# One transformer layer on one core: table products in four strips, values of the dilated sample attention a step earlier, and the last scores of the selected attention ahead of the seventh sequence's values

## The chip, the cores and the metric

The kernel runs on one core of a Trainium2 chip. The metric is the device time of one execution in microseconds (us). The median of three runs before the change is 2094.52 us (2089.33 to 2097.07).

## The reference, cut to what matters

One layer is computed for a prompt (1024 rows of width 1024) and for eight sequences that each decode four new rows on top of 8192 cached positions. In outline:

```python
qa, ka, va, qb, kc, vc, ksl, vsl, kw, vw, gates = _mix_inputs(x, norm_attn, w_in)   # RMS norm, then x @ w_in
o_a = dilated attention over the last 2048 positions (steps 1, 4, 16), 8 heads, bias from rel_bias
o_cmp, p = attention over blocks of 64 positions, compressed by a small MLP
o_slc = attention over the 16 best blocks by p          # the "choice"
o_win = attention over the last 512 positions
x = x + [o_a, gate(o_cmp, o_slc, o_win)] @ w_out ; x = x + conv/gelu feed-forward
```

`rel_bias` has 32 buckets for 16 heads. The kernel turns it into three tables (one bias per head and distance, with a mask): a one-hot matrix of 35 rows times `rel_bias`.

## The kernel before, in words

**The order of the program.** `hybrid_step` writes one program for five engines and their queues. Its stages are `front` (norm, transposes, tables, the product with `w_in`, compression), `compressed_and_dilated` (sample and prompt attention over compressed blocks, and the sample's dilated attention), `sample_selected` (selected and window attention of the eight sequences), `prompt_attention` and `ffn`. Each engine runs its own list in order; semaphores join them. TensorE (PE) writes into eight banks of PSUM; VectorE (DVE) and ScalarE (ACT) copy the banks out.

**Opening of `front`.** Nine tiles of input rows are squared and summed (ACT, `squares`), three tiles at a time get their root (`root`), DVE scales each tile (`scaled`), PE turns each in two halves (jobs "x", L579) and ACT or DVE copies each half out (`moved`). Between them stand thirteen jobs "b" (L570): products of 512 columns of the one-hot table with the bias (16 output rows each), five ahead of tile 0, four ahead of tile 3, four ahead of tile 6, each copied out on its own. PE takes all jobs in one order over five banks; job j waits until job j-5 is copied. Afterwards SP stores the tables in scratch memory (L515 to L519) and the product with `w_in` begins (L588, L601).

**`compressed_and_dilated`.** Steps s = 0 to 11 are a loop that each engine follows. In step s PE turns the 8 key tiles of sequence s (`keys`, L1546) in two halves through two PSUM banks (`psT`), which ACT (even tiles) and DVE (odd tiles) copy out; a third tile can only be turned when the first is copied. `scores` (L1568) multiplies queries and turned keys. Four sequences form a group g. After a group: maximum (DVE), exponential (ACT), `probs(g)` (L1580, turned probabilities through the same two banks), `values(g)` (L1594, 256 small matmuls), `out(g)`. Before the change `probs` stands at steps 5 and 9 and `values` at the start of steps 6 and 10. Between these steps stand parts of the compressed attention: on DVE `prompt_maxima` and `block_probs` in step 4 (L1829 to L1843), `prompt_weights` and `choice` in step 5 (L1847 to L1871).

**Loads of that stage.** SP loads 16 items (keys or values of one sequence, 1.8 MB each in five DMAs, L167 to L172) into seven slots, in the order of `turns`: keys of sequences 0 to 5 (items 0 to 5), values 0 to 3 (items 6 to 9), keys 6 and 7 (10, 11), values 4 to 7 (12 to 15). Items 0 to 4 are loaded in `front`. Slot 5 holds a bias until `d_ab` is 2 and slot 6 another until `selected_bias` is done (`d_rp` is 4). Item i waits until item i-7 is used (`free_after`). SP's list goes on with the choice, `cache_win_k`, eight stores of the compressed output (`mixc`, L1514) and `cache_win_v`. POOL issues the first gathers of the next stage (`gather_keys`, L157), two after the last keys are turned and two after `values(1)`.

**`sample_selected`.** For each sequence b and quarter c: a gather of 1 MB of keys and one of values by POOL (L157, L2131), six buffers each; PE turns the keys (L2249), multiplies them (L2260), turns the probabilities of the sequence before (`probs`, L2270) and multiplies its values (L2288). The last step is `merge`, with the values of the last sequence.

## Time and profile before

| | |
|---|---|
| median of three runs | 2094.52 us (2089.33 to 2097.07) |
| the profiled execution | 2091.84 us, its span 2090.0 us |
| PE busy in the span | 97% |
| DVE, ACT, POOL busy | 53%, 25%, 28% |
| opening (until the product with `w_in` starts) | 0 to 40.74 us |
| rest of `front` | 40.74 to 503 us |
| `compressed_and_dilated` on PE | 503 to 613 us |
| `sample_selected` on PE | 613 to 794 us |
| `prompt_attention` and `ffn` | 794 to 2090 us |

All times of the profile come from one execution, in us from the start of its span. "Idle before" is time in which the engine did nothing ahead of a row, with what ended it; "issue" means that the profile shows nothing that it waited for. The granted clock is TensorE's, as a share of full speed.

### The profile page before, as it was taken

The numbers are of one execution on the slowest core, as the hardware profiler recorded it, in microseconds if no ns is written. First come the engines' busy times: TensorE is split into PE (matmuls) and PEld (weight loads), VectorE is DVE, ScalarE is ACT, GpSimd is POOL, SyncE is SP. The second block draws the span as 40 slices with busy tenths as digits, with TensorE's granted clock in tenths as the row PEclk, the third lists the DMA queues.
The fourth block names the chain that finished last, engine by engine and source line by source line (L and its number), as shares of the span: only waits on it lengthen the run. The fifth ranks groups of instructions, "written<-read, shape, count | busy, mean of one in ns | idle before, by whom it ended". The sixth has DMA issues, their size and how long they took to land. (4 is left out here: it accounts for less than half of the span.)

```text
span 2090.0 us, 31740 instructions
## 1 busy us (share of the span) xinstructions
PE 2030.1 (97%) x12334; PEld 1325.8 (63%) x12334; DVE 1113.5 (53%) x2524; ACT 520.4 (25%) x1140; POOL 578.9 (28%) x753
## 2 busy tenths in 40 slices
PE   7999999999989989999999999999999999999998
PEld 3445466666556666766776458888888888634443
DVE  4035455421535546777775467777776766511452
ACT  4111010101333435776675031111111111000001
POOL 2444234202025740112232441322222222304110
PEclk9999999999999999999999999999999999999999
DMA  9376677663699994233343126666665422601111
GB/s 255 118 237 258 263 289 277 242 214 124 229 365 387 419 409 162 70 92 92 93 143 112 29 81 221 221 211 213 218 205 202 142 81 62 242 4 30 43 40 41
DMA packets 154296, 373.04 MB, mean 178 GB/s; under 512 B 34885, under 2 KB 92989, under 8 KB 136093
## 3 DMA queue, kind: packets, MB, share of 16 engines
q1 hardware_dynamic: 126420, 149.63, 22.8%
q0 software_dynamic: 25472, 149.45, 18.4%
q10 hardware_dynamic: 2256, 71.94, 9.8%
q8 instruction: 99, 1.62, 0.3%
q14 instruction: 49, 0.40, 0.1%
HBM read 343.68 MB, written 98.60 MB: 212 GB/s over the span
## 5 line engine op out<-in xcount | busy, mean ns | idle before, releaser
L2981 PE MATMUL ff_ps<-ff_hx,whole_aw 128*128 128x264 f32 x2464 | 550.5, 386 | 0.8 <-DVE ff_hx L3377 0.8
L2981 PEld LDWEIGHTS ff_ps<-ff_hx,whole_aw 128*128 128x128 f32 x2464 | 467.1, 190 | 80.6 <-issue 1.2
L837 DVE STREAM_TRANSPOSE whole_space<-whole_space 128x512 f32<-128x512 f32 x256 | 155.3, 674 | 153.6 <-PE late_bank L637 153.6
L601 PE MATMUL late_bank<-in_w,in_xT 128*128 128x512 f32 (+1 forms) x512 | 201.6, 547 | 0.0
L1224 DVE CUSTOM_DVE_ANT_0 pa_L<-late_bank,whole_space 128x512 f32<-128x512 f32 (+3 forms) x288 | 141.0, 532 | 43.4 <-PE late_bank L1070 41.8
L601 PEld LDWEIGHTS late_bank<-in_w,in_xT 128*128 128x128 f32 x512 | 95.1, 191 | 95.0 <-issue 88.4
L1196 ACT ACTIVATE pa_L<-pa_L,pa_nm 128x640 f32<-128x640 f32 (+3 forms) x192 | 142.0, 741 | 47.0 <-DVE pa_nm L1236 46.7
L3007 PE MATMUL ff_ps<-ff_hx,whole_space 128*128 128x512 f32 x336 | 148.0, 593 | 0.0
L717 ACT ACTIVATE in_yout<-late_bank 128x128 f32<-128x128 f32 (+5 forms) x88 | 40.9, 479 | 380.7 <-PE late_bank L601 200.2
L3461 DVE SCALAR_TENSOR_TENSOR whole_space<-whole_space,ff_kept 128x1024 f32<-128x1024 f32 x88 | 123.1, 1399 | 3.1
L637 PE MATMUL late_bank<-whole_space 128*64 128x256 f32 (+1 forms) x1152 | 121.6, 364 | 0.0
L615 PE MATMUL late_bank<-in_xT,in_w 128*128 128x352 f32 x384 | 117.6, 463 | 0.0
L3220 ACT ACTIVATE whole_space<-whole_space 128x1056 f32<-128x1056 f32 x22 | 23.8, 1083 | 367.2 <-DVE whole_space L3463 367.2
L3007 PEld LDWEIGHTS ff_ps<-ff_hx,whole_space 128*128 128x128 f32 x336 | 63.6, 190 | 80.6 <-issue 80.6
L1091 PE MATMUL late_bank<-whole_ident,pa_L 128*128 128x128 f32 x816 | 113.4, 281 | 0.9
L1091 PEld LDWEIGHTS late_bank<-whole_ident,pa_L 128*128 128x128 f32 x816 | 87.5, 141 | 41.9 <-ACT pa_L L1196 18.4
L1111 PE MATMUL late_bank<-pa_PT,whole_space 128*64 128x128 f32 x1632 | 110.3, 279 | 0.9 <-DVE pa_tmp L1266 0.5
L637 PEld LDWEIGHTS late_bank<-whole_space 128*64 128x64 f32 x1152 | 74.8, 137 | 47.2 <-issue 13.0
L1070 PE MATMUL late_bank<-whole_space,pa_qT 64*128 64x512 f32 (+3 forms) x528 | 104.0, 498 | 0.0
L1190 ACT ACTIVATE pa_PT<-late_bank 128x512 f32<-128x512 f32 (+2 forms) x174 | 86.7, 536 | 54.4 <-PE late_bank L1091 53.4
L615 PEld LDWEIGHTS late_bank<-in_xT,in_w 128*128 128x128 f32 x384 | 71.8, 190 | 42.2 <-issue 3.8
L1111 PEld LDWEIGHTS late_bank<-pa_PT,whole_space 128*64 128x64 f32 x1632 | 87.2, 136 | 16.6 <-issue 13.0
(441 smaller groups left out, 2670.0 us busy)
## 6 DMA issues: line engine op xcount, KB each, us to landing
out_new_a_k_s<-in_cache_a_k ACTq DMA_DIRECT2D x8, 4088.0 KB
out_new_a_v_s<-in_cache_a_v ACTq DMA_DIRECT2D x8, 4088.0 KB
whole_aw<-in_w_up SPq DMA_DIRECT2D x44, 512.0 KB, 7.4
in_w<-in_w_in SPq DMA_DIRECT2D x5, 2048.0 KB, 13.0
whole_space<-in_cache_a_k SPq DMA_DIRECT2D x8, 1024.0 KB
whole_space<-in_cache_a_v SPq DMA_DIRECT2D x8, 1024.0 KB
ff_hx<-in_w_down SPq DMA_DIRECT2D x14, 512.0 KB, 4.2
whole_space<-in_x_prompt SPq DMA_DIRECT2D x12, 512.0 KB, 10.2
```

The source lines that it names most:

```text
L601: mm = pe.matmul(ps[0:n, b, 0:width], xT[:, k, t * P:t * P + n], w[:, at % WBUF, k, 0:width], start=(k == 0), stop=(k == KC - 1))
L615: mm = pe.matmul(ps[:, b, 0:n], w[:, at % WBUF, k, c * P:c * P + P], xT[:, k, r0:r0 + n], start=(k == 0), stop=(k == KC - 1))
L637: mm = pe.matmul(psH[dh * HD:dh * HD + HD, r % 2, o0:o0 + n], w1[:, kv, t16, dh, :], rows[:, dh, t, :], start=(t16 == 0), stop=(t16 == 15) ...
L837: last = dve.transpose(put[:, dh, :, k * HD:k * HD + HD].rearrange("p t (g b) -> p t g b", g=2), got[:, :, :, dh, :])
L1070: pe.matmul(psS[:, c % 2, h, 0:w], q, kT[i][r, j0 * P + k0:j0 * P + k0 + w], start=True, stop=True).then_inc(s_qk, 1)
L1091: mm = pe.transpose(psT[:, b % 3, (x - x0) * P:(x - x0) * P + P], turned, ident[:, :])
L1111: mm = pe.matmul(psO[h * HD:h * HD + HD, u % 2, 0:P], V[i][:, j0 + j, v0:v0 + HD], PT[:, u % 3, (2 * j + h) * P:(2 * j + h) * P + P], star ...
L1196: nc.scalar.activation(x, x, ACT.Exp, bias=nm[:, s, h:h + 1], scale=1.0, accum_out=sm[:, s, h:h + 1]).then_inc(s_ex, 1)
L1224: dve.tensor_tensor_reduce(L[:, u % 3, h, 512 * x:512 * x + n], psS[:, c % 2, h, 0:n], T[it % 2][:, h, SEQ - w + 512 * x:SEQ - w + 512 * x ...
L2981: mm = pe.matmul(ps[:, bank_of(x, j, g), 0:H2], aw[:, j % 2, at, k, :], hx[:, bt, k, g * H2:g * H2 + H2], start=(k == 0), stop=(k == KH - 1))
L3007: mm = pe.matmul(ps[:, b, :], a[:, k, :], wd(k0 + k)[:, c0:c0 + 512], start=(k == 0), stop=(k == KD - 1))
L3461: dve.scalar_tensor_tensor(out=out[:, 0:SEQ], in0=U[:, v, k:k + SEQ], scalar=tap(k), in1=out[:, 0:SEQ], op0=ALU.mult, op1=ALU.add)
```

## The change

Four edits, all in the order of work; no arithmetic is added or removed.

1. The thirteen table products become four jobs ahead of all tiles. Each job writes three or four products into one bank, in strips of 32 output rows, and is copied out once. The tiles follow without table jobs between them; who copies what, and when, is written out anew for ACT and DVE. The tables are stored by ten DMAs instead of seven.
2. SP loads the items in the order 5, 7, 8, 9, 10, 6, 11 to 15, and stores the choice behind item 15. `cache_win_v` is loaded behind the keys of sequence 6, ahead of `cache_win_k` and the `mixc` stores.
3. `probs(0)` moves from the end of step 5 to the end of step 4, `values(0)` from the start of step 6 into step 5, between `keys(5, 0)` and `scores(4, 1)`. Each of a group's four sequences now counts `d_pv` up, so that a slot, and the first gathers, are free after one sequence's values.
4. In `sample_selected` the last quarter's scores of the last sequence stand ahead of `values` of sequence 6; ACT copies those values out after the first two exponentials of the last sequence.

```diff
@@ front @@
+    NBJ = 4
+    jobs = [("b", m) for m in range(NBJ)]
+    first_x = len(jobs)
+    for t in range(NTILE):
+        jobs += [("x", t, 0), ("x", t, 1)]
...
+                    for k in range(job[1], len(chunks), NBJ):
+                        i, c = chunks[k]
+                        o, strip = tables[i][1] + c * CH, k // NBJ * 32
+                        mm = pe.matmul(ps[strip:strip + 32, b, :], relx[:, i, :], tab_op[:, o:o + CH], start=True, stop=True,
+                                       tile_position=(0, strip))
...
             squares(2)
             root(0)
             moved(0)
+            moved(2)
+            turned(0, 0)
             squares(3)
+            turned(1, 0)
             squares(4)
...
             squares(5)
...
             root(1)
+            turned(2, 0)
+            turned(2, 1)
+            turned(3, 0)
             squares(6)
+            turned(4, 0)
             squares(7)
             squares(8)
...
             root(2)
+            turned(5, 0)
...
+            moved(1)
             mean_square(0)
+            scaled(0)
             moved(3)
+            scaled(1)
+            turned(0)
+            scaled(2)
+            turned(1)
             mean_square(1)
+            scaled(3)
+            scaled(4)
+            turned(3)
@@ compressed_and_dilated @@
-            pool.wait_ge(d_tr, use["keys", NB - 1, NTL - 1] + 1)
-            pool.wait_ge(d_pv, 1)
+            pool.wait_ge(d_pv, 4)
             for c in range(2):
                 pre.gather_keys(pool, 0, c)
+            pool.wait_ge(d_tr, use["keys", NB - 1, NTL - 1] + 1)
             ahead.retire()
             pool.sem_inc(ops.s_retired, 1)
-            pool.wait_ge(d_pv, 2)
+            pool.wait_ge(d_pv, 5)
...
-            for i in range(5, 12):
+            for i in (5, 7, 8, 9, 10, 6, 11, 12, 13, 14, 15):
...
             sp.wait_ge(s_v, 17)
...
-            for i in range(12, 16):
-                load(i)
...
+            sp.wait_ge(d_tr, use["keys", NB - 2, NTL - 1] + 1)
+            pre.load_window(sp, "cache_win_v", pre.value, pre.s_wv)
...
-                mm.then_inc(d_pv, 1)
+                    mm.then_inc(d_pv, 1)
...
             for s in range(NB + 4):
+                if s == 10:
+                    values(1)
                 for g in range(2):
-                    if s == 6 + 4 * g:
-                        values(g)
...
                 if s < NB:
                     keys(s, 0)
+                if s == 5:
+                    values(0)
                 if 1 <= s <= NB:
                     scores(s - 1, 1)
...
-                    if s == 5 + 4 * g:
+                    if s == turning[g]:
                         probs(g)
@@ sample_selected @@
-                    if 0 <= n < NB * NQ:
+                    if 0 <= n < NB * NQ - 1:
                         scores(n // NQ, n % NQ)
+                    if n == NB * NQ - 2:
+                        scores(NB - 1, NQ - 1)
...
```

`turning` is (4, 9). ACT's and DVE's parts of `probs` move with it; DVE's copy of `probs(0)` then stands between its key copies of step 4 and `prompt_maxima`.

## Rows read from the trace of the kernel before

**Rows 1.** The page: busy time of the engines in the span.
```profile
PE 2030.1 (97%) x12334; PEld 1325.8 (63%) x12334; DVE 1113.5 (53%) x2524; ACT 520.4 (25%) x1140; POOL 578.9 (28%) x753
```
**Rows 2.** Timeline of PE in the opening: start, us, instruction, count, idle before.
```profile
24.77 3.60 PE L570 MATMUL late_bank<-in_yout,in_relx 35*16 35x512 f32 x8
28.30 2.84 PE L579 MATMUL late_bank<-whole_ident,whole_space 128*128 128x128 f32 x24
31.07 4.51 PE L570 MATMUL late_bank<-in_yout,in_relx 35*16 35x512 f32 x8
35.51 4.66 PE L579 MATMUL late_bank<-whole_ident,whole_space 128*128 128x128 f32 x24
40.74 3.64 PE L588 MATMUL late_bank<-in_w,in_xT 128*32 128x512 f32 x16 [0.57 <-ACT in_xT L717]
```
**Rows 3.** Timelines of ACT and of DVE in the opening.
```profile
14.70 1.04 ACT L724 ACTIVATE sample_kcs<-whole_space 128x1024 f32<-128x1024 f32 x1
...
16.59 3.68 DVE L799 SCALAR_TENSOR_TENSOR whole_space<-whole_space,in_rstd,sel_BS 128x1024 f32<-128x1024 f32 x3 [0.27 <-ACT in_rstd L729]
...
24.22 0.68 DVE L803 TENSOR_SCALAR in_xT<-late_bank 128x512 f32<-128x512 f32 x1
```
**Rows 4.** Timeline of PE, `compressed_and_dilated`, steps 3 to 5.
```profile
539.71 1.00 PE L1546 MATMUL late_bank<-whole_ident,whole_space 128*128 128x128 f32 x8 [0.25 <-ACT sample_turned L1739]
...
550.80 0.99 PE L1546 MATMUL late_bank<-whole_ident,whole_space 128*128 128x128 f32 x8 [1.13 <-ACT sample_turned L1739]
...
554.15 3.41 PE L1546 MATMUL late_bank<-whole_ident,whole_space 128*128 128x128 f32 x16
...
564.36 8.14 PE L1594 MATMUL late_bank<-whole_space,cd_PT 128*32 128x128 f32 x256
```
**Rows 5.** Timeline of DVE, same steps: first and last of two groups.
```profile
551.92 1.21 DVE L1829 TENSOR_REDUCE cd_mxp<-cd_Lp 128x64 f32<-128x1024 f32 x1
...
554.73 0.48 DVE L1843 TENSOR_SCALAR cd_early<-cd_early,cd_rcs 128x128 f32<-128x128 f32 x2
...
564.19 1.20 DVE L1847 TENSOR_REDUCE cd_smp<-cd_Lp 128x64 f32<-128x1024 f32 x1
...
569.41 0.22 DVE L1871 TENSOR_SCALAR cd_pen<-cd_score 64x128 f32<-64x128 f32 x1
```
**Rows 6.** Stretches of 5 us: PE, PEld, DVE, ACT, POOL busy, clock, DMA share, GB/s.
```profile
525.00:530.00 5.00, 5.00 (x100) 3.55 (x96) 0.69 (x1) 1.05 (x2) 0.00 (x0) 1.00 0.00 0
...
565.00:570.00 5.00, 5.00 (x170) 4.07 (x160) 4.31 (x15) 0.00 (x0) 0.00 (x0) 1.00 0.03 7
...
655.00:660.00 5.00, 4.27 (x105) 3.89 (x94) 0.53 (x1) 0.97 (x3) 1.21 (x2) 1.00 0.48 197
...
785.00:790.00 5.00, 4.00 (x121) 3.43 (x124) 3.29 (x10) 0.31 (x1) 0.00 (x0) 0.97 0.42 172
```
**Rows 7.** Timeline of SP's queue: items 6 and 12, first rows.
```profile
531.30 1.84 SPq L167 DMA_DIRECT2D whole_space<-in_cache_a_v  x3
...
570.37 1.99 SPq L167 DMA_DIRECT2D whole_space<-in_cache_a_v  x3
```
**Rows 8.** Timeline of POOL: the first gather of the next stage.
```profile
588.85 1.01 POOL L157 DMA_INDIRECT whole_space<-in_cache_slc_k,sample_idx  x1 [72.91 <-PE late_bank L1546]
```
**Rows 9.** Timeline of PE: second part of `values(1)`, window keys, first keys that waited.
```profile
606.93 5.43 PE L1594 MATMUL late_bank<-whole_space,cd_PT 128*32 128x128 f32 x117 [2.79 <-issue]
...
614.06 4.02 PE L2185 MATMUL late_bank<-whole_ident,whole_space 128*128 128x128 f32 x32
...
637.92 3.19 PE L2249 MATMUL late_bank<-whole_ident,whole_space 128*128 128x128 f32 x16 [2.25 <-DMA whole_space<-in_cache_slc_k,sample_idx]
```
**Rows 10.** Timelines of PE and of POOL: end of `sample_selected`.
```profile
778.41 1.06 PE L2260 MATMUL late_bank<-whole_space,sample_Qb 128*32 128x512 f32 x8
781.63 3.76 PE L2270 MATMUL late_bank<-whole_ident,sb_work 128*128 128x128 f32 x16 [2.15 <-ACT sb_work L2413]
...
779.29 0.94 POOL L2131 DMA_INDIRECT whole_space<-in_cache_slc_v,sample_idx  x1 [15.12 <-PE late_bank L2291]
```

More of the change, by code:

```diff
@@ L267, in front @@
     chunks = [(i, c) for i, (_, _, ln) in enumerate(tables) for c in range(ln // CH)]
-    shares = [chunks[0:5], chunks[5:9], chunks[9:13]]
-    jobs = []
-    for g in range(NG):
-        jobs += [("b", i, c) for i, c in shares[g]]
-        for t in range(3 * g, 3 * g + 3):
-            jobs += [("x", t, 0), ("x", t, 1)]
+    NBJ = 4
+    segments = []
+    for k, (i, c) in enumerate(chunks):
+        if c == 0 or k % NBJ == 0:
+            segments.append([i, c, k // NBJ, k % NBJ, 0])
+        segments[-1][4] += 1
+    NTS = len(segments) + A0 // FARW
+    jobs = [("b", m) for m in range(NBJ)]
+    first_x = len(jobs)
+    for t in range(NTILE):
+        jobs += [("x", t, 0), ("x", t, 1)]
     NX = len(jobs)
@@ L294, in front @@
     span_of = {ch: [j for j, x in enumerate(jobs) if x[0] in "nsq" and x[1] == ch] for ch in range(6)}
-    first_x = {g: min(j for j, x in enumerate(jobs) if x[0] == "x" and x[1] == 3 * g) for g in range(NG)}
     last_b = max(j for j, x in enumerate(jobs) if x[0] == "b")
@@ L299, in front, with by_act @@
     kT_row = {0: 0, 2: 8, 3: 10}
-    on_act = [j >= NX or j % 2 == 0 for j in range(NJ)]
+    def by_act(j):
+        if j < first_x:
+            return j % 2 == 0
+        return j >= NX or jobs[j][2] == 0 or jobs[j][1] % 3 == 2
+    on_act = [by_act(j) for j in range(NJ)]
     def done(j):
@@ L690, in copy_out @@
             if job[0] == "b":
-                _, i, c = job
-                o = res_at[i] + c * CH
-                return copy(res[:, o:o + CH], ps[0:HA + HB, b, :], 1.0)
+                n = 32 * len(range(job[1], len(chunks), NBJ))
+                return copy(res[0:n, job[1] * CH:job[1] * CH + CH], ps[0:n, b, :], 1.0)
             if job[0] == "x":
@@ L755, in _, with turned @@
             nc.scalar.activation(bias[:, 0:1], bias[:, 0:1], ACT.Sqrt)
+            def turned(t, h):
+                moved(first_x + 2 * t + h)
             squares(0)
@@ L856, in _, with turned @@
             dve.wait_ge(s_one, 2)
+            def turned(t):
+                moved(first_x + 2 * t + 1)
+            moved(1)
             mean_square(0)
-            for t in range(3):
-                scaled(t)
-            moved(1)
+            scaled(0)
             moved(3)
+            scaled(1)
+            turned(0)
+            scaled(2)
+            turned(1)
             mean_square(1)
-            for t in range(3, 6):
-                moved(2 * t - 1)
-                scaled(t)
-            moved(11)
-            moved(13)
-            mean_square(2)
-            for t in range(6, 9):
-                moved(2 * t + 3)
-                scaled(t)
-            for j in range(21, NX, 2):
-                moved(j)
+            scaled(3)
+            scaled(4)
+            turned(3)
+            scaled(5)
+            turned(4)
+            mean_square(2)
+            scaled(6)
+            scaled(7)
+            turned(6)
+            scaled(8)
+            turned(7)
             indices()
@@ L905, in _ @@
             pool.memset(ss[:, :], 1.0).then_inc(s_one, 1)
+            pool.memset(relx[:, :, HA + HB:32], 0.0).then_inc(s_one, 1)
             pool.memset(w2, 0.0).then_inc(s_wz, 1)
```

62 lines of the change are left out of this document (30 added, 32 removed).

## The prediction

> **What bounds the kernel now.** I read the page first, then stretches of 5 us of the two sample stages, then the timelines of single engines where PE or the DMA engines pause. PE is busy 97% of the span [rows 1], so a change of order can win only at its pauses, at its stretches of low clock, or where the DMA engines dictate. Three places are touched.
>
> In the opening PE is not what ends it. Tile 3 is scaled by DVE before PE has finished the second batch of table products, which runs until 28.4, and tile 6 waits in the same way until 35.5; then the last three tiles take until 40.2 and the product with `w_in` starts at 40.74 [rows 2]. From there to 503 us PE has no pause to speak of, so what the opening wins should go through.
>
> In `compressed_and_dilated` PE is near its limit: small waits for a bank, and one of 1.13 us after which keys ran slowly, 3.41 us for sixteen transposes [rows 4] where 32 others took 4.02 [rows 9]. The DMA engines pause twice: at 525 to 530 and at 565 to 570 nothing moves [rows 6]. With their flanks these pauses are 10.6 us and 9.8 us (idle shares of the 5 us stretches around those two, summed). The first ends when SP is let past item 6 at 531.30, the second when item 12 goes out at 570.37, behind the choice [rows 7]. From about 580 on the DMA engines are full until the gathers end, but for 2.6 us at 655 to 660 [rows 6]. So the end of `sample_selected` is the end of a stream of bytes: it moves by the pauses filled or made, not by how early one load is issued.
>
> **The change part by part, against the profiled execution, 2091.84 us (2.7 us under the median of the runs).**
>
> *Opening.* Two batches of 3.60 and 4.51 us leave PE's list between tiles [rows 2]. The four strips of a job should overlap: 16 matmuls of L588 with 32 output rows took 3.64 us [rows 2], 0.23 us each, where eight of L570 took 3.60, 0.45 each, although L588 ran right after an idle stretch, at a low clock. Four jobs ahead of the tiles then take about 7 us from 9.93, done before the first tile is scaled at 17.8, so they are hidden; the cover is the wait for the input rows. What remains is a chain of ACT and DVE. Nine squares at 1.04, scaling at 1.2 a tile (3.68 for three) and copies of 0.6 to 0.7 [rows 3], followed through the new lists by hand: root 1 at 24.4, tiles 3 to 5 scaled by 29.7; squares 6 to 8 now stand behind copies and end at 31.7, root 2 at 32.2, tile 8 scaled at 36.6, copied at 38.1. The product starts at 38.4 instead of 40.74: -2.3. If PE's transposes all ran at the low clock (twice the 2.84 for three tiles' 24 [rows 2]) they would take 1.9 us a tile, and it would be about -1. I take -2, ends -3 and 0. Three more table stores on SP, and a memset on POOL, lie beside 60 us in which nothing waits for them: nothing.
>
> *Step 4.* DVE now waits in its list for `probs(0)` before `prompt_maxima` and `block_probs`. Those are 3.3 us in one piece, 551.92 to 555.21 [rows 5], done so far while PE worked on scores and on keys of step 5. Now they start near 556.5 and end near 560. PE can turn three tiles of `keys(5)`, then needs DVE's copy of the second: it stands from about 558 to 560.5. +2.5 us, ends 0 and +3.3.
>
> *Step 5.* `prompt_weights` and `choice` are 5.4 us of DVE, 564.19 to 569.63 [rows 5], and lay wholly under `values(0)`, 8.14 us from 564.36 [rows 4]. With `values(0)` moved ahead of `keys(5, 1)` DVE idles under it, then has these 5.4 us, the scaling of the output (0.75) and a key copy (0.7) in front of PE's fourth tile of `keys(6)`. Behind `keys(5, 1)` PE has 0.95 of scores, 1.0 of block sums and three tiles, 1.6: 3.5 us. It stands 6.9 - 3.5 = +3.4 us; ends 0 (if the lists slip past each other) and +4.
>
> *Clock.* After the pause of 1.13 us sixteen transposes took 1.4 us too long [rows 4]; after one of 2.79 the 117 matmuls of `values(1)` took 5.43 instead of about 3.9 [rows 9]. Two new pauses can cost up to 3 us, or nothing beyond what is slow there already: +1.5.
>
> *Loads.* Items 7, 8 and 9 fill the first pause, 520 to 535; item 10 must wait for the keys of sequence 3, turned at 540.7 [rows 4], and item 6 stands behind it: about 5 us of new pause. Item 11 is in by 557; item 12 needs the keys of sequence 5, which PE now turns after `values(0)`: near 571 to 575. The two early gathers (at 588.85 before [rows 8]) go out when `values(0)` is done, near 568 to 570, and cover 5 us. That leaves 12 us empty. Later there may be 3 us more while SP waits for the choice to be read back. The sum of pauses is about 20, as it was (20.4): the loads are moved, not gained. Nothing for them, ends -3 and +3.
>
> *Start of `sample_selected`.* PE arrives 2.5 + 3.4 + 1.5 = 7.4 us later in its own account. It had waited there for gathered keys, 2.25 us [rows 9] and 0.5 more, with 1.6 us lost to the low clock behind it (3.19 for 2.0, and 0.4 on the scores). These 4.3 us it need not wait again. So +7.4 - 4.3 = +3.1 at the point where its first values free buffers for POOL, which is where the 2.6 us of DMA pause lie [rows 6]; this swallows the rest. The stream ends about +3.
>
> The second part of `values(1)` was held for 2.79 us by "issue", with the DMA engines full; `values(0)`, the same 256 matmuls with the DMA engines empty, ran through in 8.14 [rows 4, 9]. In the new order `values(0)` meets them empty again and `values(1)` full again, since window loads and `mixc` stores lie just ahead. I leave both as they are.
> The Trainium skill (Runtime: NRT & Kernel Launch, Instruction fetch mechanics) says that an engine's instructions come in blocks of 256 over a DMA queue of its own; by this the pause is a late block, and would go, 2.8 us, only if the DMA engines had room at that place. The trace fits with it, but shows no block.
>
> *Tail.* With the last scores ahead of `values` of sequence 6, the wait of 2.15 us before the last `probs` [rows 10] and its slow 3.76 us (some 2.0 for sixteen at full clock) could go: -3.9 at best. But the last two value gathers are released by the end of those values, at 779.29 [rows 10], and now 1.1 us later; they were landing until about 787 (0.42 of the stretch from 785 [rows 6]). The last values would start near 782 and wait for them. I take -1.5, ends -3.9 and +1.
>
> Sum: -2 + 3 - 1.5 = -0.5 us; 2091.84 becomes about 2091.3. The runs' median stands 2.7 higher; I write 2092.
>
> **The rivals.** *The pauses shrink.* If DVE's two blocks of work slip into gaps, if `values(1)` finds its instructions in time (2.8 and 1.5 of clock), and with -3 and -3.9 at the ends, the time is 2091.84 - 3 - 4.3 - 3.9 + 0 = about 2080.5. For it: both DMA pauses are real, and the gathers do start 20 us earlier. Against it: the 5.4 us of DVE need a cover of PE work that is no longer there. The rule on instruction blocks belongs here.
>
> *DVE becomes the bound in steps 4 to 6.* Both waits at full size and each followed by some 3 us at 1.2 GHz instead of 2.4: 3.3 + 4 + 3 = 10.3 us; if the item loads behind them are late by as much, nothing of the 4.3 comes back, and with an opening and a tail of nothing it is 2102. It decides if `keys(6)` begins after 583, against 572.5, the end of `values(0)`, before [rows 4]. For it: two PSUM banks and one order on DVE leave no way round. Against: 7 to 8 us of the DMA backlog at 613 are there to absorb it.
>
> *The strips do not overlap.* Thirteen products one after another at the low clock, 1.74 each, would end at 32.5, and the tiles would follow from there: about +11, 2103. L588 speaks against it, though it has 128 rows of operand and not 35.
>
> **How the numbers follow.** Near nothing (2086 to 2098): 0.53. Pauses shrink: 0.24, of which three quarters lie beyond 0.5% (10.5 us, about what a measurement of this kernel can tell from no change). DVE the bound: 0.18, nearly half of it beyond. Strips: 0.05, all beyond. That gives faster 0.19, slower 0.13, same 0.68. For eight in ten I reach into both neighbours, 2082 to 2101: the ends of the unsure terms alone (loads 3 either way, clock 1.5, opening 1 to 2, tail 2.5) make some 6 us each way.
>
> **What would show it.** In the changed kernel: L588 starts at 38 to 39; PE stands before the fourth tile of `keys(5)` for 2 to 3 us, ended by DVE, and again before the fourth of `keys(6)` for about 3.4; `prompt_weights` starts after `values(0)` and not under it; the DMA engines are empty for about 12 us before 570; no keys of L2249 wait more than 1 us before 650; in the tail the wait before the last L2270 is gone and one of 1 to 2 us stands inside the last L2288. I am wrong if `keys(6)` begins before 575, or if PE reaches the window keys (614.06 before [rows 9]) more than 3 us earlier.

## The result, and the profile after

Six runs of the changed kernel gave 2102.9 us in the median (2102.49 to 2108.17), six of the kernel before, on the same chip, 2092.5 (2087.34 to 2097.07): ratio 1.005, 95% interval 1.0032 to 1.0068, so 0.5% slower, about 10.4 us. The forecast was 2092, with a range that ended at 2101. The profiled run took 2103.95 us, its span is 2102.2, 12.2 more than before. The page's line of busy times answers to [rows 1]:

```profile
PE 2030.0 (97%) x12334; PEld 1330.5 (63%) x12334; DVE 1115.1 (53%) x2517; ACT 519.4 (25%) x1138; POOL 578.7 (28%) x754
```

PE is busy for as long as before in total, so the 12.2 us are time in which it stands.

The opening went as forecast. The timeline of PE (start, us, instruction, count, idle before), first the row of the kernel before at the same place, which [rows 2] lack:

```profile
9.93 8.71 PE L570 MATMUL late_bank<-in_yout,in_relx 35*16 35x512 f32 x10 [9.93 <-DMA in_relx<-in_c_pick]
```

In the changed kernel:

```profile
10.56 7.04 PE L581 MATMUL late_bank<-in_yout,in_relx 35*32 35x512 f32 x26 [10.56 <-DMA in_relx<-in_c_pick]
...
37.69 3.64 PE L600 MATMUL late_bank<-in_w,in_xT 128*32 128x512 f32 x16 [0.56 <-ACT in_xT L728]
```

The strips overlap: 13 products (26 halves) take 7.04 us, 0.54 each, where the first five took 8.71, 1.74 each. The product with `w_in` starts at 37.69 instead of 40.74 [rows 2]; of these 3.05 us, 2.0 are left at the first keys of the dilated stage (500.92 against 502.93).

From there all is lost again. PE in steps 4 to 6 and up to the window keys:

```profile
555.42 0.70 PE L1572 MATMUL late_bank<-whole_ident,whole_space 128*128 128x128 f32 x4
556.34 1.14 PE L1572 MATMUL late_bank<-whole_ident,whole_space 128*128 128x128 f32 x8 [0.21 <-DVE cd_PT L1946]
560.15 1.11 PE L1572 MATMUL late_bank<-whole_ident,whole_space 128*128 128x128 f32 x4 [2.67 <-DVE sample_turned L1762]
561.19 10.27 PE L1620 MATMUL late_bank<-whole_space,cd_PT 128*32 128x128 f32 x256
...
582.25 0.66 PE L1572 MATMUL late_bank<-whole_ident,whole_space 128*128 128x128 f32 x4 [3.17 <-DVE sample_turned L1762]
...
625.05 0.39 PE L2207 MATMUL late_bank<-whole_ident,sample_knew 32*128 32x32 f32 x2 [4.27 <-DMA whole_space<-in_cache_win_k]
625.37 6.29 PE L2213 MATMUL late_bank<-whole_ident,whole_space 128*128 128x128 f32 x32
```

The two waits for DVE stand where the forecast had them, 2.67 and 3.17 us. New is the line before the last: PE waits 4.27 us for `cache_win_k` and begins the window keys 11 us later than before [rows 9]; there it waited for nothing. `values(0)`, 8.14 us before [rows 4], takes 10.27 after its pause.

The stretches of 5 us (PE, PEld, DVE, ACT, POOL busy, clock, DMA share, GB/s):

```profile
535.00:540.00 5.00, 4.62 (x39) 2.92 (x41) 2.13 (x4) 1.94 (x4) 0.00 (x0) 0.99 0.00 2
...
560.00:565.00 5.00, 4.85 (x72) 3.58 (x76) 0.78 (x2) 0.00 (x0) 0.00 (x0) 0.50 0.01 2
565.00:570.00 5.00, 5.00 (x152) 4.14 (x156) 0.00 (x0) 0.00 (x0) 0.00 (x0) 0.92 0.01 3
570.00:575.00 5.00, 4.75 (x74) 2.77 (x63) 0.69 (x1) 0.60 (x1) 1.99 (x2) 1.00 0.21 39
...
600.00:605.00 5.00, 4.91 (x18) 1.51 (x17) 2.70 (x5) 1.81 (x3) 0.00 (x0) 1.00 0.46 125
...
625.00:630.00 5.00, 4.95 (x24) 4.91 (x25) 1.61 (x3) 1.26 (x3) 1.44 (x2) 0.50 0.70 250
630.00:635.00 5.00, 5.00 (x69) 3.68 (x68) 1.66 (x4) 2.46 (x4) 1.92 (x3) 0.93 0.20 32
```

Two things are to be read here. The DMA pause of before at 525 to 530 [rows 6] is filled, but the last column but one shows new ones: the idle shares of all stretches from 520 to 605, summed, are 26.6 us, against 20.5 before, and 5.5 more follow at 625 to 635. (The 2.6 us of before at 655 to 660 [rows 6] are gone; from 520 to 665 the sums are 32.3 and 23.4.) And the clock column shows 0.50, that is 1.2 of 2.4 GHz, in two stretches behind pauses of PE: `values(0)` and the 32 transposes of the window keys (6.29 us instead of the 4.02 of [rows 9]) run slowly.

The pause at 625 to 635 is made by PE's lateness. The window keys lie in buffers that the next gathers need, and POOL waits for their transposes:

```profile
632.47 0.97 POOL L157 DMA_INDIRECT whole_space<-in_cache_slc_k,sample_idx  x1 [6.04 <-PE late_bank L2213]
```

Why the window keys are late is in SP's queue. Before, it had these rows:

```profile
569.65 0.67 SPq L1502 DMA_DIRECT2D scr_pen<-cd_pen  x1
...
588.00 1.74 SPq L151 DMA_DIRECT2D whole_space<-in_cache_win_k  x2
```

In the changed kernel:

```profile
575.39 2.20 SPq L167 DMA_DIRECT2D whole_space<-in_cache_a_v  x3
...
592.67 0.66 SPq L1529 DMA_DIRECT2D scr_pen<-cd_pen  x1
601.48 0.56 SPq L140 DMA_DIRECT2D sample_kcs<-scr_pen  x1
...
604.21 1.05 SPq L151 DMA_DIRECT2D whole_space<-in_cache_win_k  x2
```

Item 12 goes out at 575.39 (570.37 before [rows 7]). The penalties' store, which stood ahead of item 12, now stands behind item 15, at 592.67, and it is 8.8 us later that SP, which waits for it to land, reads the choice back. `cache_win_k` is issued 16.2 us later than before.

In the tail the wait before the last `probs` is gone, as forecast, but inside the last values there are two:

```profile
797.99 1.08 PE L2316 MATMUL late_bank<-whole_space,sb_PT 128*32 128x128 f32 x32 [1.48 <-DMA whole_space<-in_cache_slc_v,sample_idx]
801.07 1.71 PE L2316 MATMUL late_bank<-whole_space,sb_PT 128*32 128x128 f32 x32 [2.00 <-DMA whole_space<-in_cache_slc_v,sample_idx]
...
804.88 3.62 PE L2340 MATMUL late_bank<-sb_stackW,sample_vcs 128*128 128x32 f32 x16 [0.72 <-DVE sb_stackW L2549]
```

and the last line, 1.97 us in the kernel before, is slow behind them. From the last keys to the first product of the prompt's attention it takes 25.1 us, 22.4 before.

### The profile page after: what moved, and what is told of

Its sections match the earlier page's. It is cut to its first block and busy times, and to the rows that moved or that the text cites. A ratio compares the mean times of both kernels' runs of the same rounds, so it can differ in the third digit from the quotient of the medians.

```text
span 2102.2 us, 31736 instructions
## 1 busy us (share of the span) xinstructions
PE 2030.0 (97%) x12334; PEld 1330.5 (63%) x12334; DVE 1115.1 (53%) x2517; ACT 519.4 (25%) x1138; POOL 578.7 (28%) x754
## 5 line engine op out<-in xcount | busy, mean ns | idle before, releaser
L1117 PEld LDWEIGHTS late_bank<-whole_ident,pa_L 128*128 128x128 f32 x816 | 87.3, 141 | 42.1 <-ACT pa_L L1222 18.2
L1137 PE MATMUL late_bank<-pa_PT,whole_space 128*64 128x128 f32 x1632 | 110.3, 279 | 0.9 <-DVE pa_tmp L1292 0.5
```

The source lines that it names most:

```text
L1117: mm = pe.transpose(psT[:, b % 3, (x - x0) * P:(x - x0) * P + P], turned, ident[:, :])
L1137: mm = pe.matmul(psO[h * HD:h * HD + HD, u % 2, 0:P], V[i][:, j0 + j, v0:v0 + HD], PT[:, u % 3, (2 * j + h) * P:(2 * j + h) * P + P], star ...
```

## Experiments

All 15 were timed against the kernel before on the same chip, but not all on one chip: e1 to e4, e5 to e8, e9 to e12 and e13 to e15 are four groups. Inside a group medians can be compared; across groups, and with the changed kernel, only the ratios. The window keys' begin is the clearest mark in the traces. Since the profiled executions reach the dilated stage up to 5 us apart, I count in this section from the first keys of `compressed_and_dilated` in each trace (502.93 before, 500.92 changed). "out(1)" is the begin of PE's last product ahead of the window keys, which takes 0.66 us; if the window keys begin later than 0.6 us behind it, PE waited for their load.

| kernel | ratio to before (95%) | median, us | choice read back | out(1) | window keys begin | prompt attention begins |
|---|---|---|---|---|---|---|
| before | 1 | 2090.2 to 2092.5 | 82.5 | 110.3 | 110.9 | 291.1 |
| changed | 1.0050 (1.0032, 1.0068) | 2102.9 | 100.6 | 119.2 | 124.1 | 307.5 |
| e1 opening alone | 0.9984 (0.9970, 0.9999) | 2088.1 | 81.3 | 107.8 | 108.4 | 291.3 |
| e2 tail alone | 1.0010 (0.9998, 1.0023) | 2094.5 | 81.7 | 110.0 | 110.5 | 295.0 |
| e3 sample stages alone | 1.0049 (1.0032, 1.0066) | 2100.6 | 97.4 | 116.9 | 121.3 | 301.1 |
| e4 loads alone | 0.9982 (0.9969, 0.9995) | 2087.5 | 87.7 | 109.5 | 110.1 | 286.9 |
| e12 e4, item 12 held | 1.0039 (1.0022, 1.0055) | 2098.5 | 95.0 | 106.2 | 118.7 | 298.1 |
| e5 changed, POOL stores pen | 1.0016 (1.0000, 1.0032) | 2094.9 | 87.2 | 117.1 | 117.7 | 298.5 |
| e6 changed, DVE covered | 1.0047 (1.0029, 1.0066) | 2099.5 | 93.7 | 109.5 | 118.7 | 299.4 |
| e8 e5 and e6 | 1.0028 (1.0015, 1.0042) | 2096.9 | 84.9 | 109.7 | 116.2 | 299.2 |
| e7 changed, values(0) back | 1.0037 (1.0026, 1.0048) | 2098.6 | 94.2 | 113.5 | 118.0 | 301.3 |
| e11 changed, win_k first | 1.0023 (1.0010, 1.0037) | 2095.9 | 97.3 | 117.4 | 117.9 | 301.6 |
| e13 changed, gathers late | 1.0068 (1.0056, 1.0081) | 2107.3 | 95.1 | 117.3 | 124.4 | 308.3 |
| e14 e8 and e11 | 0.9986 (0.9975, 0.9998) | 2088.1 | 85.6 | 110.9 | 111.4 | 290.4 |
| e9 opening and loads | 0.9983 (0.9965, 1.0000) | 2085.9 | 86.5 | 108.9 | 109.5 | 288.3 |
| e10 e9, spare buffers | 0.9966 (0.9952, 0.9979) | 2083.6 | 87.4 | 108.4 | 109.0 | 283.4 |
| e15 e10, POOL stores pen | 0.9943 (0.9928, 0.9958) | 2081.4 | 86.2 | 109.9 | 110.5 | 285.0 |

**The parts alone.** e1 has the hunks of `front` only, e2 those of `sample_selected`, e3 those of `compressed_and_dilated`. e4 is e3 with PE's order as before:

```diff
-        turning = (4, 9)
+        turning = (5, 9)
...
-                if s == 10:
-                    values(1)
                 for g in range(2):
+                    if s == 6 + 4 * g:
+                        values(g)
...
-                if s == 5:
-                    values(0)
```

> The kernel before with only the new opening (table products in four jobs, new copy order). Theory (the loss lies in the dilated stage and the tail): L588 starts near 37.7 as it did after the whole change, instead of 40.74, and the gain of 2 to 3 us goes through, since nothing downstream was seen to wait for it: 2 to 3 us under the kernel before. Rival 'the opening costs later' (its earlier start is eaten by projections that wait for loads, so that the whole change's loss is not the dilated stage's alone): no difference, within 1 us, or slower.

> The kernel before with only the last scores ahead of the seventh sequence's values. Theory (the last two value gathers are released by the end of those values, so the last values wait for them and the low clock follows): last probs start without a wait, but 1 to 2 us waits stand inside the last values, and the stretch from the last keys to the start of prompt_attention is 24 to 25 us instead of 22.4: 1.5 to 3 us slower. Rival 'the tail is a gain, and its loss in the whole change is what the late stream of gathers brought' : 1.5 to 4 us faster.

> The kernel before with only the changes in the two sample stages (loads in another order and PE's probs(0) and values(0) a step earlier), opening and tail as before. Theory: this holds the loss; window keys some 13 us later than before (no 2 us from the opening), a wait of about 4 us for the window keys' load, last keys of sample_selected 11 to 14 us later, and the time 9 to 12 us over the kernel before, of which perhaps 2 come back in the tail. With the two others it should add up to the whole change's +10.4: -2.5 + 10 + 2.5. Rival 'the parts do not add' (two of them meet on one resource): under 6 us here.

> The kernel before with the new order of the dilated loads, the early gathers, the penalties' store behind item 15 and the window values' load ahead, but with PE's probs(0) and values(0) in their old places and DVE's lists as before; opening and tail as before. Theory 'DVE lost its cover' as the first cause: no waits for DVE of 2.7 and 3.2 us, values(0) under which prompt_weights and choice lie again, and the loss is less than half of the previous experiment's: 0 to +4 us. Rival 'the chain of penalties and window loads, or the loads' order, is the cause': the window keys still wait about 4 us for their load and the time is 5 to 10 us over the kernel before.

The sample stages hold the loss: e3 is 9.7 us over the kernel before in medians. The opening wins 2.8. The tail alone is not told from no change by its runs (1.0010, interval from 0.9998), but its trace shows the waits, 1.63 and 2.67 us, and 26.2 us from the last keys to the prompt's attention instead of 22.4. Medians of the three parts add up to -2.8 + 9.7 + 3.6 = +10.5, the change's own 10.4.

e4 was the surprise: the load order alone is a gain, 3.4 us. All the loss comes in with PE's new order. The window keys do not wait, and the choice is read back 5.2 us later than before without harm. SP's queue in e4:

```profile
561.29 1.83 SPq L167 DMA_DIRECT2D whole_space<-in_cache_a_v  x3
...
590.16 0.57 SPq L140 DMA_DIRECT2D sample_kcs<-scr_pen  x1
...
592.88 1.12 SPq L151 DMA_DIRECT2D whole_space<-in_cache_win_k  x2
```

Item 12 goes out at 561.29, when PE has turned the keys of sequence 5, and 58.8 us behind the first keys; in the changed kernel it is 74.5.

**Repairs of the changed kernel, one at a time.** e5 lets POOL issue the penalties' store:

```diff
@@ gpsimd @@
                 pre.gather_keys(pool, 0, c)
+            pool.wait_ge(s_v, 17)
+            pool.dma_start(bass.AP(scr["pen"].tensor, 0, [[P, NB], [NB * P, 8], [1, P]]), pen[:, :]).then_inc(s_out, 16)
@@ sync @@
-            sp.wait_ge(s_v, 17)
-            sp.dma_start(bass.AP(scr["pen"].tensor, 0, [[P, NB], [NB * P, 8], [1, P]]), pen[:, :]).then_inc(s_out, 16)
             sp.wait_ge(s_out, 16)
```

e6 moves DVE's blocks under the early `values(0)`, e7 moves `values(0)` behind step 5, e8 is e5 and e6 together:

```diff
@@ e6, vector @@
+                if s == 5:
+                    prompt_maxima()
+                    block_probs()
+                    prompt_weights()
                 if s < NB:
                     key_copies(dve, dve.tensor_copy, d_cd, 1, s, 1)
...
-                if s == 4:
-                    prompt_maxima()
-                    block_probs()
                 if s == 5:
-                    prompt_weights()
                     choice()
@@ e7, tensor @@
-                if s == 10:
-                    values(1)
+                if s in (6, 10):
+                    values(s // 10)
...
-                if s == 5:
-                    values(0)
```

> The changed kernel, with the store of the choice's penalties issued by POOL behind the two early gathers, as soon as DVE has made them, instead of by SP behind item 15. DVE's waits stay as they are. Theory 'DVE first, then the chain': the two waits for DVE (2.67 and 3.17 us) stay, SP reads the choice back right behind item 15 instead of 8.8 us later, cache_win_k is issued near 595 instead of 604 and the wait of 4.27 us at the window keys is gone with most of the low clock behind it: 2096 to 2099, 3.5 to 7 us under the changed kernel. Rival 'the chain is all of it': 2090 to 2094. Rival 'bytes decide' (the window load lands when the DMA engines get to it): within 1.5 us of the changed kernel.

> The changed kernel, with prompt_maxima, block_probs and prompt_weights moved on DVE to just behind the first key copies of step 5, so that they run under the early values(0). PE's order and the loads are as in the changed kernel. Theory: the wait of 2.67 us before the fourth tile of keys(5) is gone and the one of 3.17 us in keys(6) falls under 1, with less low clock; keys(6) begins near 573; but the penalties are still stored behind item 15 and the window keys' load lands only some 3 us earlier, so PE's wait there grows to about 5 us, and the gain over the changed kernel is 2 to 5 us: 2098 to 2101. Rival 'DVE's waits are all of it': 2090 to 2095, and no wait at the window keys.

> The changed kernel, with PE's values(0) back behind all of step 5; probs(0) stays in step 4, and the loads' order stays. Theory: item 12 takes the buffer of the keys of sequence 5, and these are now turned before values(0), so it goes out near 564 instead of 575; prompt_weights and choice lie under values(0) again; the wait of 2.67 us stays and the one of 3.17 is gone; the DMA engines are not empty for 12 us; everything behind is 6 to 10 us earlier, with no wait at the window keys: 2093 to 2097. Rival 'probs(0) ahead of prompt_maxima is the costly part': 2099 to 2102.

> Both repairs, of e5_pen and e6_cover, in the changed kernel; values(0) stays early. Theory: the two causes are most of the loss of the dilated stage (13 us against the loads alone), and what is left is item 12's lateness (575 instead of 561) and the tail: 2091 to 2096. Rival 'the late item 12 is a third of its own size': 2097 to 2101, with PE waiting for the last items' loads or for the window keys although both repairs work as meant.

e6 is the run that unseats my first suspect. The waits for DVE are gone, and PE pays at the window keys instead:

```profile
555.66 0.66 PE L1572 MATMUL late_bank<-whole_ident,whole_space 128*128 128x128 f32 x4 [0.29 <-DVE sample_turned L1762]
556.24 8.14 PE L1620 MATMUL late_bank<-whole_space,cd_PT 128*32 128x128 f32 x256
...
573.18 0.66 PE L1572 MATMUL late_bank<-whole_ident,whole_space 128*128 128x128 f32 x4 [1.18 <-DVE sample_turned L1762]
...
618.60 0.39 PE L2207 MATMUL late_bank<-whole_ident,sample_knew 32*128 32x32 f32 x2 [8.51 <-DMA whole_space<-in_cache_win_k]
```

`values(0)` is back at 8.14 us, PE ends its own work 9.7 us earlier on the common count (109.5 against 119.2), and then it waits 8.51 us; the interval of its ratio covers the changed kernel's. e5 is the mirror: no wait at the window keys, but PE comes late by its own account (117.1). So two chains run side by side to the window keys, PE's and the bytes', and either repaired alone leaves the other. e5 gained a little more than expected, 7.1 us by the ratios; e6 gained 0.6, which is inside the noise.

e8 should have been near the kernel before (2091 to 2096); it came out at 2096.9, at the edge of its rival: its choice is read back at 84.9, its window keys begin at 116.2, behind a wait of 5.84 us. The bytes ahead of them are still too many, as e11 and e14 bear out below. e7 missed its range (2098.6): item 12 goes out 65.1 us behind the first keys, against 74.5, but DVE's first wait (2.52 us) stays and PE waits 3.83 us for the window keys.

In the five kernels in which SP stores the penalties behind item 15 and loads `cache_win_v` ahead of `cache_win_k`, with the gathers early, and PE waits (changed, e3, e6, e7, e12), the window keys begin 23.6 to 25.0 us behind the reading back of the choice: the landing hangs on that point of the queue.

**The late item alone, and the order of the bytes.** e12 is e4 with one wait more, e11 the changed kernel with the two window loads swapped, e13 the changed kernel with the early gathers late:

```diff
@@ e12, sync @@
+                if i == 12:
+                    sp.wait_ge(d_pv, 2)
@@ e11, sync @@
-            sp.wait_ge(d_tr, use["keys", NB - 2, NTL - 1] + 1)
-            pre.load_window(sp, "cache_win_v", pre.value, pre.s_wv)
             sp.wait_ge(d_tr, use["keys", NB - 1, NTL - 1] + 1)
             pre.load_window(sp, "cache_win_k", pre.key, pre.s_wk)
+            pre.load_window(sp, "cache_win_v", pre.value, pre.s_wv)
@@ e13, gpsimd @@
+            pool.wait_ge(d_tr, use["keys", NB - 1, NTL - 1] + 1)
             pool.wait_ge(d_pv, 4)
             for c in range(2):
                 pre.gather_keys(pool, 0, c)
-            pool.wait_ge(d_tr, use["keys", NB - 1, NTL - 1] + 1)
```

> The kernel with the loads alone changed (e4), and SP held at item 12 until values(0) has multiplied its second sequence, near 568.5 instead of 561.3, as late as in the change without the opening; PE's and DVE's orders as before. This is the price of the late item alone. Theory: the stream of bytes up to the window keys shifts by about 7 us, PE, which had at most 3 us to spare there, waits 3 to 6 us for cache_win_k and runs its 32 transposes at the low clock behind it: 4 to 8 us over e4, that is 1 to 5 over the kernel before. Rival 'only DVE's waits cost, the late item is absorbed': within 2 us of e4.

> The changed kernel with cache_win_k loaded ahead of cache_win_v, nothing else. Theory 'bytes ahead of the window keys': 2 MB less in front of them at some 380 GB/s is 5 us, so the load lands near 620, the wait of 4.27 us and the 2.3 us of low clock go, and the time is 3 to 6 us under the changed kernel: 2097 to 2100, 5 to 8 over the kernel before. Rival 'the issue is late, not the bytes' (the store and the reading back of the penalties): the window keys still wait over 3 us and the gain is under 2 us.

> The changed kernel with the two early gathers held back until the keys of sequence 7 are turned, as in the kernel before; nothing else. Theory: the two gathers are 2 MB that share the DMA engines with the items ahead of the window loads; without them the choice is read back some 4 us earlier (597 instead of 601.5), but held back they are served beside the window keys' load, so its landing, 23 to 25 us behind the reading back in all runs with that order, is the same or 1 to 3 us earlier: within 3 us of the changed kernel, 2100 to 2103. Rival 'the early gathers are what makes the window keys late': no wait for cache_win_k, 2096 to 2098.

e12 is the cleanest of them. Nothing of PE's or DVE's order differs from e4; item 12 goes out at 568.21 instead of 561.29, and the kernel goes from 0.9982 to 1.0039 of the time before, 12 us, more than I expected. Its PE timeline:

```profile
564.05 8.14 PE L1596 MATMUL late_bank<-whole_space,cd_PT 128*32 128x128 f32 x256
...
599.17 8.71 PE L1596 MATMUL late_bank<-whole_space,cd_PT 128*32 128x128 f32 x256 [0.88 <-ACT cd_PT L1741]
...
621.18 0.39 PE L2181 MATMUL late_bank<-whole_ident,sample_knew 32*128 32x32 f32 x2 [11.77 <-DMA whole_space<-in_cache_win_k]
621.50 5.21 PE L2187 MATMUL late_bank<-whole_ident,whole_space 128*128 128x128 f32 x32
```

PE has no wait for DVE, is even early, and stands 11.77 us. A late item load is enough to make most of the loss of e3 (12 of the 14 us between e4 and e3 by the ratios; the intervals of e12 and e3 overlap). What follows it in SP's queue (three more items, the penalties' store and its return, 2 MB of window values) is all ahead of the window keys. The delay of 6.9 us in the issue became 7.3 in the reading back of the choice and 8.6 in the begin of the window keys.

e11 shows the bytes: with 2 MB less ahead of them, the window keys do not wait, and 6.2 us of their delay are gone (117.9 against 124.1), what is left being PE's own chain (117.4). Not all 6.2 are the bytes': in that trace item 12 goes out 2.8 us earlier than in the changed kernel's, for `values(0)` ran at full clock (8.14 us), and the choice is read back 3.3 us earlier. At 23.6 us or more behind the reading back, as in the five kernels above, the keys would have landed 3 us later than PE took them.

e13 went against a third suspect. With the gathers late the choice is read back 5.5 us earlier (2.8 of these because item 12 itself goes out earlier in that trace), and still the window keys begin no earlier, 29.3 us behind it. That fits with the gathers being served beside their load now, as expected. The runs are above the range expected, and no faster than the changed kernel, rather slower (1.0068, the intervals overlap): the early gathers are not the cause.

**All repairs, and the best version.** e14 is e8 with e11's swap, and keeps `values(0)` early. e9 is e1 and e4 together. e10 adds the early last scores to e9, with the last two gathers in spare buffers, and e15 adds e5's store to e10.

```diff
@@ e10, sample_selected @@
+        SPARE = {30: 2, 31: 0}
+        def value(n):
+            return pre.key(SPARE[n]) if n in SPARE else pre.value(n % NSV)
...
-                if n >= NSV:
+                if n in SPARE:
+                    pool.wait_ge(s_tr, use["keys", (n - 4) // NQ if n == 30 else (n - 1) // NQ, 2, 3] + 1)
+                elif n >= NSV:
                     pool.wait_ge(s_pv, (n - NSV) // NQ + 1)
...
-                    pe.wait_ge(s_vl[n % NSV], 16 * (n // NSV + 1))
+                    if n in SPARE:
+                        pe.wait_ge(s_kl[SPARE[n]], 16 * (n - 24))
+                    else:
+                        pe.wait_ge(s_vl[n % NSV], 16 * (n // NSV + 1))
```

> The two parts that won alone, together: the new opening and the new order of loads, with PE's steps in sample stages and tail as in the kernel before. Theory: they touch different stretches and add up, -2.8 and -3.4 in medians: 5 to 7 us under the kernel before, 0.9965 to 0.9975. Rival 'what the opening gives is lost at the gathers', whose stream of bytes ends when it ends: 3 to 4 us under it.

> The previous kernel, and the last scores early as in the change, with the last two value gathers put into two key buffers that are free by then, so that they are released by the turned keys near 757 and 767 instead of by the end of the seventh sequence's values. Theory (the early scores are a gain of up to 3.9 us, which the late release of these two gathers took back): no wait inside the last values over 0.5 us, no low clock behind, prompt_attention begins 3 to 4 us earlier than in the previous kernel: 2.5 to 4 us under it. Rival 'the DMA engines are full there anyway': the keys of the last sequence come later by what the two gathers take, and the gain is under 1 us.

> The changed kernel with all three repairs: DVE's blocks under values(0), penalties stored by POOL, cache_win_k ahead of cache_win_v. values(0) stays ahead of the second half of keys(5) and item 12 stays late. Theory: two chains run side by side to the window keys, PE's own and the bytes'; with both shortened PE reaches them at about 610 and finds them landed by 611 to 613: no wait over 3 us, 2090 to 2094, that is 9 to 12 us under the changed kernel and level with the kernel before, for the tail's 3 us and the opening's -3 cancel. Rival 'bytes behind the late item set it whatever their order': a wait of 5 us or more, 2095 to 2098.

> The kernel of the spare buffers (e10) with the penalties stored by POOL behind the two early gathers, so that the choice is read back before the items' loads are done and the DMA pause near 590 is filled. Theory: PE waits for nothing there, so only the gathers at the end can profit, where PE waits 1.0, 1.9 and 1.8 us for keys: 0 to 2 us under e10. Rival 'POOL's wait for the penalties delays its own gathers' : 1 us or more over e10.

e14 confirms the two chains: PE's ends near 111, no wait for the bytes', and the time is 2088.1, 2 us better than expected and some 13 us under the changed kernel by the ratios. PE's new order need cost nothing once its followers are mended. How much of the 13 us is DVE's cover is not isolated, since no run has the other two repairs without it; but in e5 and e11, which lack it, PE's own chain ends at 117.1 and 117.4.

e9's two gains add up less than fully: -4.3 in medians, between the theory's 5 to 7 and the rival's 3 to 4. In e10 the tail becomes what the change had meant it to be:

```profile
773.19 2.83 PE L2324 MATMUL late_bank<-whole_space,sb_PT 128*32 128x128 f32 x96
776.24 1.08 PE L2324 MATMUL late_bank<-whole_space,sb_PT 128*32 128x128 f32 x32 [0.22 <-DMA whole_space<-in_cache_slc_v,sample_idx]
```

One wait of 0.22 us is left of the two. POOL had issued the last two gathers at 754.51 and 757.96, where the changed kernel issues them at 791.87 and 793.11:

```profile
754.51 0.93 POOL L2164 DMA_INDIRECT whole_space<-in_cache_slc_v,sample_idx  x1 [0.30 <-issue]
757.96 0.94 POOL L2164 DMA_INDIRECT whole_space<-in_cache_slc_v,sample_idx  x1 [2.52 <-PE late_bank L2282]
```

From the last keys to the prompt's attention it takes 19.4 us (23.5 in e9, 25.1 in the changed kernel). The runs show 2.3 us of it between the medians of e9 and e10, and the intervals of the two overlap. e15 is the fastest, 2081.4 us, 0.9943 (0.9928 to 0.9958) of the time before, so 10 to 12 us under the kernel before and over 20 under the changed one. Its 2.2 us under e10 come from another group of runs, with overlapping intervals, so that step alone is not shown.

**The idle time of the DMA engines over the whole stage.** The sums given with the profile stop at 665. The table has the idle shares of stretches of 2 us, summed from 17 to 271 us behind the first keys of each trace (the whole stream of loads and gathers but its last few), and beside them the begin of the last keys of `sample_selected`, on the same count. (A share over 1 counts as no idle time.)

| kernel | idle DMA time, us | last keys begin |
|---|---|---|
| before | 23.9 | 268.7 |
| e4 | 18.2 | 264.5 |
| e14 | 20.8 | 266.6 |
| e5 | 28.1 | 272.3 |
| e12 | 29.8 | 275.6 |
| e3 | 32.8 | 278.7 |
| changed | 36.8 | 282.4 |

In all sixteen other kernels, against the kernel before, the last keys move by what the idle time moves, within 1.5 us; the begin of the window keys is off by up to 3.9. The prediction's rule, that the end of `sample_selected` is the end of a stream of bytes and moves by the pauses, holds. The two chains say where pauses come from: in e12, against e4, 7.5 of the 11.6 us more are ahead of the window loads, while the stream stands for item 12, and 4.1 come later, behind the late window keys.

## Why the prediction was wrong

*Opening.* Right: -2 forecast, -2.0 at the first keys in the profile, -2.8 in e1's runs. The rival "The strips do not overlap" fell with the row of 7.04 us above. It put the 1.74 us of a product down to the low clock; the clock column shows 1.00 from 10 to 18 us in both kernels, so why the first products are that slow stays open.

*Steps 4 and 5.* Right in place and size: +2.5 and +3.4 forecast, 2.67 and 3.17 measured. But e6 shows what they were worth: removed, they gave 9.7 us on PE's own account with the low clock behind them, and hardly anything in the time, for PE waited for bytes then.

*Clock.* The term of 1.5 us was too small: `values(0)` alone lost 2.1, and the window keys' transposes 2.3, behind a pause that was not forecast. Against these stand 1.55 us that the second part of `values(1)` won back (3.88 instead of 5.43 [rows 9]).

*Loads.* This is the step that failed. The text put item 12 at 571 to 575 (575.39), the DMA pause ahead of it at about 12 us, and then counted idle DMA time, 20 against 20.4: "the loads are moved, not gained. Nothing for them". This term was put at nothing and is most of the miss: over the stage the idle time rose by 12.9 us, and on the common count the last keys came 13.7 later, where the forecast had about +3 for the end of the stream. The rule was right and its sum was wrong. Up to 605 the sum was 26.6, not 20: the pause at 535 to 545 took 6.9 us instead of 5, the one ahead of item 12 some 15 instead of 12. And the sum held only the pauses among this stage's own loads, so that what late loads do to the next stage was not in it: PE late at the window keys, their buffers late, the gathers late, 5.5 us at 625 to 635.

For that the text would have had to ask who stands last in the queue. `cache_win_k` now stands behind the late item, the penalties' way to memory and back, and 2 MB of window values, and PE needs it first. Before, it was issued at 588.00 and landed by the profile's median 21.6 us later, at 609.6, 4.4 us ahead of PE: that slack should have been a row and a bound. "Later there may be 3 us more while SP waits for the choice to be read back" names the place, but as idle DMA time, and not as 16 us for the load behind it. e12 prices the late item alone at 12 us of time; e11 prices the place of `cache_win_v` at 5.6 and e5 the store's place at 7.1, by the differences of the ratios. Such prices need not add, since each shortens the same chain only until PE's own is the longer: e5 and e6 gave 7.1 and 0.6, and e8, with both, 4.6.

*Start of `sample_selected`.* "These 4.3 us it need not wait again" was right as an observation (the waits for gathered keys are gone from there), but it was set against a lateness of 7.4 us that was 13.2 on the common count at the window keys.

*Tail.* -1.5 forecast, +2.7 in the profile: 4.2 us more of the miss. The mechanism was named (the last two gathers are released by the end of the seventh values, and later now); the term was taken from the middle of its range, where the row of their landing near 787 stood at its bad end. The release was the cause: in e10, where it is moved (and the bytes end earlier too), the two waits of 1.48 and 2.00 us are down to one of 0.22.

*The rivals.* "DVE becomes the bound in steps 4 to 6" gave 2102, nearest to the time, and its clause "if the item loads behind them are late by as much" is what came true. That the number fell near is luck. Its cause is not: in e6 DVE is not the bound and the time is 2099.5. "The pauses shrink" describes e4 and e9, which keep PE's old order; that the loads alone are a gain of 3.4 us I had not seen.

*The instruction blocks.* The prediction left `values(1)` as it was; it was interrupted by "issue" again, 1.80 us instead of 2.79 [rows 9]. The experiments say more, below.

## What to carry to other kernels

Where a stage is bound by its bytes, the sum of the idle DMA time is the right account, but it must run to the end of the stream and hold the pauses that late loads make further on. To find those, write down for each load that an engine will need soon its issue, its landing, the time of its first use, and what stands ahead of it in its queue; where a margin goes below nothing, a later pause follows. A step moved forward on one engine moves another one back, and its buffers with it: here one item load, released 7 us late, cost 12. When two chains meet at one point, a repair of one of them can show nothing by itself (e6, 0.6 us); try it together with the others before calling its cause harmless.

## What the runs showed of the hardware

The pauses of PE called "issue" inside the 256 matmuls of `values` go with the DMA engines' load, though not without exception. `values(0)` ran through in 8.14 us where these were idle (0.03 of the stretch [rows 6]; also in e6, and in e12 up to 568), and was interrupted in e4, e9, e10 and e15, where they were full or nearly so. In e4:

```profile
564.16 5.54 PE L1594 MATMUL late_bank<-whole_space,cd_PT 128*32 128x128 f32 x174
571.00 2.99 PE L1594 MATMUL late_bank<-whole_space,cd_PT 128*32 128x128 f32 x82 [1.30 <-issue]
```

The exception is e7: its `values(0)` ran in one piece, in 8.61 us, though the engines were at 0.88 and more from 568 on; they had been idle just before. `values(1)` was interrupted for 1.45 to 2.79 us in every kernel but e12, each time behind the 139th of its matmuls. In e12 the DMA engines had a gap just ahead of it:

```profile
595.00:597.00 2.00, 1.91 (x5) 0.73 (x5) 0.78 (x2) 1.23 (x3) 0.00 (x0) 1.00 0.54 195
597.00:599.00 2.00, 1.28 (x9) 0.74 (x7) 0.86 (x4) 1.08 (x2) 0.00 (x0) 1.00 0.17 20
```

The changed kernel had such a gap too, but 7 us ahead (0.06 of 600 to 602, `values(1)` from 608.90), and was interrupted.

The DMA view of these stretches lists a queue of kind "instruction" beside the data queues. That fits with what the Trainium skill says (Runtime: NRT & Kernel Launch, Instruction fetch mechanics), that an engine's instructions come in blocks of 256 over a DMA queue of their own. By this, and it is my inference, a block is late when the data queues are full while it is fetched; the fixed place in the list speaks for it. The runs vary the load and not the fetching itself, so the link is likely and not shown; each interruption took 0.65 to 2.79 us.

The granted clock fell from 2.4 to 1.2 GHz behind some pauses and not behind others, and their length alone does not tell which. Where PE had stood for 1.93 to 2.79 us inside `values(1)` (before, e2, e5, e14), the 117 matmuls behind took 5.43 us (mean clock 0.78 from 605 to 610 before); where it had stood for 1.45 to 1.84 us (the changed kernel and eleven others) they took 3.87 or 3.88. But `values(0)` took 10.27 us behind a pause of 2.67 us in the changed kernel, and 8.14 behind one of 2.70 us, at the same place of the same list, in e5; in e3 and e13, behind shorter ones of 2.36 and 2.29 us, it took 9.03 and 9.11. A term for the low clock is better kept as a range than as a mean: here a pause cost from nothing to 2.6 us (the window keys in e6, 6.58 us instead of 4.02).
